# An encoder trunk with expert layers: neighbouring weight rows to one partition

## What is computed

```python
def expert_choice_ffn(h, router, w_gate, w_up, w_down):
    cap = CAPACITY_FACTOR * T // N_EXPERTS          # 64 of 512 tokens, 32 of 256
    aff = jax.nn.softmax((xt @ router).astype(jnp.float32), axis=-1)
    gate, idx = lax.top_k(aff.T, cap)
    xe = xt[idx]
    hid = jax.nn.silu(jnp.einsum('ecd,edf->ecf', xe, w_gate)) * jnp.einsum('ecd,edf->ecf', xe, w_up)
    ye = jnp.einsum('ecf,efd->ecd', hid, w_down) * gate[..., None].astype(h.dtype)
    out = jnp.zeros_like(xt).at[idx.reshape(-1)].add(ye.reshape(-1, D))
```

## Time and profile before

| | |
|---|---|
| Time, median of three runs | 2625.58 us (2623.7 to 2633.08) |
| Span of the profiled execution | 2622.3 us, from the first to the last instruction |
| TensorE products busy | 2317.6 us, 88% |
| TensorE weight loads busy | 1748.5 us, 67% |
| VectorE busy | 1461.6 us, 56% |
| ScalarE busy | 1288.2 us, 49% |
| GpSimd busy | 319.5 us, 12% |
| DMA | 503.33 MB, mean 192 GB/s |
| Expert slabs | 384 loads of 1024 KB |

### The profile page before, as it was taken

The page is one execution under the profiler, slowest core; times in us unless marked ns, Lnnn a source line. Parts: engine busy times, 40 slices in busy tenths (PEclk is TensorE's granted clock), DMA queues, the critical chain, the costliest instruction groups (busy, mean ns, idle before and its releaser), DMA issues. The chain is left out here.

```text
span 2622.3 us, 32854 instructions
## 1 busy us (share of the span) xinstructions
PE 2317.6 (88%) x11472; PEld 1748.5 (67%) x11472; DVE 1461.6 (56%) x2096; ACT 1288.2 (49%) x1591; POOL 319.5 (12%) x198
## 2 busy tenths in 40 slices
PE   6999997999866999999982998989894999999993
PEld 3777865676764777777761887878773677777772
DVE  2212233334335889888873233343424888988883
ACT  2312214344224777777754323342422677777774
POOL 0000000000010211122202212121002111122210
PEclk9999997999967999999995999999895999999997
DMA  4110111000075999999943201010026899999983
GB/s 172 28 55 13 54 56 74 20 10 10 24 294 196 369 389 386 384 387 384 387 156 112 104 26 38 22 54 6 1 106 268 315 393 388 386 385 386 386 336 116
DMA packets 138376, 503.33 MB, mean 192 GB/s; under 512 B 14807, under 2 KB 23383, under 8 KB 136004
## 3 DMA queue, kind: packets, MB, share of 16 engines
q1 hardware_dynamic: 131140, 477.26, 47.6%
q0 software_dynamic: 7168, 25.17, 4.1%
HBM read 471.59 MB, written 32.31 MB: 192 GB/s over the span
## 5 line engine op out<-in xcount | busy, mean ns | idle before, releaser
L1552 DVE TENSOR_TENSOR w_lo<-arena,w_hi 128x2048 fp32r<-128x2048 f32 x378 | 860.7, 2289 | 150.8 <-ACT w_hi L1547 147.6
L1547 ACT ACTIVATE w_hi<-arena 128x2048 fp32r<-128x2048 f32 x384 | 735.5, 1917 | 287.4 <-PE pT_ps L1566 110.7
L581 ACT ACTIVATE arena<-proj_ps 128x384 f32<-128x384 f32 (+3 forms) x78 | 38.0, 487 | 369.4 <-PE proj_ps L557 244.6
L402 PE MATMUL score_ps<-arena 128*128 128x256 f32 (+6 forms) x576 | 179.5, 436 | 30.6 <-ACT arena L508 11.2
L425 PE MATMUL o_ps<-arena 128*128 128x64 f32 (+1 forms) x1360 | 164.3, 265 | 15.7 <-DVE arena L487 9.6
L1566 PE MATMUL proj_ps<-w_hi,x_hi 128*96 128x512 f32 x512 | 164.6, 403 | 11.0 <-DVE x_lo L1684 6.2
L500 ACT ACTIVATE arena<-pT_ps 128x512 f32<-128x512 f32 (+3 forms) x172 | 90.6, 527 | 166.7 <-PE pT_ps L413 166.2
L1566 PE MATMUL pT_ps<-w_hi,h_hi 128*96 128x512 f32 x512 | 163.4, 400 | 9.2 <-DVE h_lo L1688 9.2
L425 PEld LDWEIGHTS o_ps<-arena 128*128 128x128 f32 (+1 forms) x1360 | 152.4, 183 | 28.1 <-issue 19.9
L1566 PE MATMUL proj_ps<-w_hi,x_lo 128*96 128x512 f32 x512 | 161.7, 397 | 0.0
L1566 PE MATMUL proj_ps<-w_lo,x_hi 128*96 128x512 f32 x512 | 161.5, 396 | 0.0
(11 more groups left out here) (178 smaller groups left out, 4108.4 us busy)
## 6 DMA issues: line engine op xcount, KB each, us to landing
arena<-w_gate SPq DMA_DIRECT2D x128, 1024.0 KB, 8.5
arena<-w_up SPq DMA_DIRECT2D x128, 1024.0 KB, 9.3
arena<-w_down SPq DMA_DIRECT2D x128, 1024.0 KB, 8.3
arena<-w_c SPq DMA_DIRECT2D x12, 1024.0 KB, 4.8
arena<-w_out SPq DMA_DIRECT2D x2, 4096.0 KB, 12.1
arena<-w_a SPq DMA_DIRECT2D x2, 3072.0 KB, 13.0
residual_rows<-x SPq DMA_DIRECT2D x12, 512.0 KB, 2.6
normed_rows<-arena SPq DMA_DIRECT2D x12, 512.0 KB, 3.4
```

What stands on the lines that cost most here:

```text
L402: last = pe.matmul(score_ps[:u.nq, j % 2, u.cols(i)], q(u, h), k(u, h), start=True, stop=True)
L581: return eng.activation(dst, src(bank), ACT.Copy, scale=1.0 if scale is None else scale)
L1547: act.activation(w_hi[:, self.part_slot(run, i)], self.raw[:, slot], ACT.Copy).then_inc(self.w_hi, 1)
L1552: dve.tensor_tensor(w_lo[:, slot], self.raw[:, self.raw_slot(run, i)], w_hi[:, slot].bitcast(F32), ALU.subtract).then_inc(self.w_lo, 1)
```

## The change

A partition of a slab takes two neighbouring rows of the matrix, which lie together in memory (8 KB), and no longer the rows `p` and `p + 128` of the slab. The transposes take every second channel of a block of 256 to match (`rows_of`), for the tokens and for the hidden rows. The gains that `dve_x` uses are laid out in the same order in 16 more columns of `gcol`, which the host fills; to make room `rden` becomes another name of `den`.

```diff
-        gcol = sb("gcol", [P, 37])
+        gcol = sb("gcol", [P, 53])
         gq, gkv = gcol[:, 32:35], gcol[:, 35:37]
+        g_moe = [gcol[:, 37:45], gcol[:, 45:53]]
...
-        rden = sb("rden", [P, 16, AH])
+        rden = den
...
+            def rows_of(self, a, c):
+
+                return a[:CAP].rearrange("t (s p j) -> t s j p", s=NS, j=SL)[:, c // SL, c % SL]
+
             def load(self, sp, run, e, i, first=False):
...
-                sp.dma_start(self.raw[:, slot], src[s * SL * P:(s + 1) * SL * P, :].rearrange("(c p) n -> p c n", p=P)
+                sp.dma_start(self.raw[:, slot], src[s * SL * P:(s + 1) * SL * P, :].rearrange("(p c) n -> p c n", p=P)
                              ).then_inc(self.w_in[slot], 16)
...
-                        sp.dma_start(self.raw[:, slot], w_down[l, NE - 1, s * SL * P:(s + 1) * SL * P, :].rearrange("(c p) n -> p c n", p=P)
+                        sp.dma_start(self.raw[:, slot], w_down[l, NE - 1, s * SL * P:(s + 1) * SL * P, :].rearrange("(p c) n -> p c n", p=P)
...
-                    last = pe.transpose(o_ps[:, c // 4, (c % 4) * CAP:(c % 4 + 1) * CAP], self.xe[:CAP, c * P:(c + 1) * P], ident[:CAP, :CAP])
+                    last = pe.transpose(o_ps[:, c // 4, (c % 4) * CAP:(c % 4 + 1) * CAP], self.rows_of(self.xe, c), ident[:CAP, :CAP])
...
-                    last = pe.transpose(o_ps[:, c // 4, (c % 4) * CAP:(c % 4 + 1) * CAP], self.hid[:CAP, c * P:(c + 1) * P], ident[:CAP, :CAP])
+                    last = pe.transpose(o_ps[:, c // 4, (c % 4) * CAP:(c % 4 + 1) * CAP], self.rows_of(self.hid, c), ident[:CAP, :CAP])
...
-                g = g_of[f"ffn{l}"]
+                g = g_moe[l]
...
+    def slabs(g):
+
+        return a(g).reshape(NS, P, SL).transpose(1, 0, 2).reshape(P, DC)
+
...
-                                 column(g_qa[0]), column(g_kva[0])], axis=1),
+                                 column(g_qa[0]), column(g_kva[0]), slabs(ln_ffn_g[0]), slabs(ln_ffn_g[1])], axis=1),
```

## The result

The changed kernel took 2639.14 us (median of four, 2636.17 to 2644.3), the kernel before 2624.85 us beside it: a ratio of 1.0054, 95% interval 1.0031 to 1.0076. It is slower by 14 us. The profiled executions span 2634.3 and 2622.3 us.

What follows compares the result with a forecast made beforehand. TensorE alone was taken to bound the expert stages. Only SyncE's earlier end in layer 1 counted, all other terms 0: 2625.58 - 0.95 = 2624.6 us, own range 2620 to 2632, 8-in-10 range 2611 to 2645.

Steps and rivals of the forecast that it cites:

- its own sign: Expert loop: the prediction is wrong if the expert period moves over 0.4 us or ScalarE comes to wait for a landing.
- rival A: Expert transposes: strided weight loads set the pace; 18.4 us more (2644) at half price, 53.8 (2679) at full; chance 0.12.
- What bounds the kernel: Both expert stages: TensorE alone, 34.57 us an expert; no engine waits for DMA, and transfers do not slow its products.
- Loads: 384 expert slab loads, from 256 runs of 4 KB to 128 of 8 KB: priced at nothing in the loop.
- SyncE before the routing: End of norm stage: fewer runs let all twelve loads fit the queue; layer 1 gains 0.95 us, layer 0 nothing.
- Gain columns and reciprocals: Larger gain load at the start and 140 in-place reciprocals: both taken as 0, the reciprocals with upper bound 3.5 us.
- Transposes: 512 expert transposes at step two: 23 ns more per weight load, hidden by 33 ns free, so 0; bound 53.8 us.
- B: Expert loop: the DMA loads did hold it back, so the change is faster, about 2612 us; chance 0.04.
- C: Start of routing: with TensorE at 2.4 GHz in the norm stage, 7.5 us gained (2618), up to 15 (2611); chance 0.09.
- D: Loads and SyncE's issue: queue counts bytes or rows still travel by 4 KB, so nothing shows, 2625.6 us; chance 0.09.

Runs made afterwards that it cites:

- e2: The changed kernel with both transposes put back to plain, keeping 8 KB loads, gain columns and in-place reciprocal: 2622.13 us, ratio 0.9988 to the kernel before.
- e3: The kernel before with only its transposes changed, to read every fourth column of a block of 512: 2642.21 us, one run.
- e4: Changed kernel with plain transposes; ScalarE and VectorE reorder by reading at step two, host reorders gains and router rows: 2629.16 us, ratio 1.0010 to the kernel before.
- e8: Changed kernel with stepped transposes standing singly between products of down's first slab and the next gate's first slab: 2630.68 us, ratio 1.0026 to the kernel before.

## Why the prediction was wrong

The forecast was 2624.6 us, its own range 2620 to 2632, and measured were 2639.14. By its own sign it fails too: the expert period moved by 0.54 us, more than 0.4. The wider range holds the time only because its upper end, 2645, was taken from rival A, which had a chance of 0.12.

- What bounds the kernel: right. TensorE's chain, the waits without a DMA, the same 231 ns a product.
- Loads: right, at nothing in the loop; the packets went as said.
- SyncE before the routing: right in what it gives; 0.95 us in layer 1, none in layer 0. Ten loads of 128 runs left before the issue slowed, where six of 256 had, so runs count for more than bytes here; but not all twelve fitted, as the prediction had it: the last two took 1.4 and 2.3 us.
- Gain columns and reciprocals: right; e2 has both and an expert of 34.57 us. The reciprocals take 160 and 166 ns in place too, so the 25 ns of the upper bound were those of the wider shape.
- **Transposes: the step that failed.** The sentences were "a third of the way from one to four is 46 ns" and "I expect half of the 46 ns, 23, which the free 33 ns hide". The price is not spread between step one and four: in the turns step two costs 71 ns more (212 against 141), nearly all of the 76 that step four does (217, e3). The half price came out, 138 / 2 = 69 ns, though its reason, that the turn handles a column once, was not tested and why a step lengthens the load stays open. The cover came out too: 212 - 92 = 120 ns of pace from the earlier trace rows, against 0.92 / 8 = 115 measured. Rival A had just this sum, 36 ns and 18.4 us; measured are 15.1 us in the loops, since a group of eight lengthens by 0.26 us, 33 ns a transpose, and the experts at the ends of a layer add little: from a layer's first turn to its last it is 7.4 us more in layer 0 and 8.1 in layer 1, 15.5 in all.
- The other rivals. B fell with e2: 8 KB loads leave the expert at 34.57 us. C did not come: the last 32 router products took 6.85 us in the changed kernel and in e2 as before, at the lower clock. D fell with the packets and the 0.95 us.
- The Trainium skill (Advanced Engine Details and Errata, section SBUF Cachelines) holds that two hits on a 16-byte line hide its latency. Here two fp32 hits on a line (step two, 212 ns) cost as much as one (step four, 217; step eight, 202). For a weight load at 2.4 GHz the measurement decides against the rule as I used it. e4 says little on it: its stepped reads of PSUM are not reads of SBUF, and its stepped row scalings, which do read SBUF, took 83 ns more on 1135.

What misled me was filling a gap between two measured points with a straight line, and letting a rule that agreed lower the chance of the one rival that was priced right.

## What to carry to other kernels

A load on a saturated engine's path is priced with the cover that it has: here 33 ns were free, 71 were added, and each of eight in a row showed 33. If rows must be re-ordered, do it where an engine reads in its slack (e4) or between long products (e8, 98 to 99 ns a transpose against 115), not in a run of short transposes; neither beat the kernel before. And larger transfers gave nothing to this loop, in which no engine waits for a landing.

## What the runs showed of the hardware

A weight load of a transpose (128 columns, fp32) takes 141 ns at step one and 202 to 217 ns at steps two, four and eight when the granted clock is 1.00. At 0.50 it takes 218 to 226 ns at any of these steps, so a step costs something at the higher level alone. ScalarE (1004 ns) and VectorE (1207 ns) read PSUM at step two for nothing. In the short norm stage of layer 1 TensorE can run at either level of its clock: a block of 16 router products took 1.86 us in e2's execution, 3.43 in e4's and 3.44 in e3's, and the stage's last products ended 6.6 us apart in e2 and e4.
